# Unread products of the identity on TensorE at the stage borders of a two-layer decoder step

## The reference

```python
for l in range(DEPTH):                       # DEPTH = 2
    if l % 2 == 0:                           # gated linear recurrence and causal pooling
        hp, ... = hgrn_pool_mixer(yp, ...)
    else:                                    # sliding-window attention, 16 heads, 2 kv heads
        hp, ... = swa_mixer(yp, ...)
    yp = post_norm(yp, hp, ...)              # layer_norm(ALPHA * x + h)
    mk, mv = mem_kv(mem_prompt, mem_wkv[l])  # 256 memory tokens
    yp = post_norm(yp, cross_attn(yp, mk, mv, mem_wq[l], mem_wo[l]), ...)
    yp = post_norm(yp, peer_ffn(yp, ...), ...)
```

## Times and profile before

| | before |
|---|---|
| median of 3 runs | 2371.53 us (2364.65 to 2371.93) |
| the profiled execution's own time | 2373.22 us |
| its span | 2371.5 us |
| mean granted clock of TensorE over the span | 0.981 |
| PE busy | 2256.0 us, 95% |
| DVE busy | 1674.4 us, 71% |
| ACT busy | 1301.6 us, 55% |
| POOL busy | 1003.5 us, 42% |

### The profile page before, as it was taken

The page is one execution under the profiler, slowest core; times in us unless marked ns, Lnnn a source line. Parts: engine busy times, 40 slices in busy tenths (PEclk is TensorE's granted clock), DMA queues, the critical chain, the costliest instruction groups (busy, mean ns, idle before and its releaser), DMA issues. The chain is left out here.

```text
span 2371.5 us, 45604 instructions
## 1 busy us (share of the span) xinstructions
PE 2256.0 (95%) x15467; PEld 2039.7 (86%) x15467; DVE 1674.4 (71%) x3386; ACT 1301.6 (55%) x2953; POOL 1003.5 (42%) x777
## 2 busy tenths in 40 slices
PE   7899899999999999999989898999999999999998
PEld 7788699999999977888878787999999998778886
DVE  4667489969898656666646555899698884566666
ACT  4324365456776555555546544644677764555554
POOL 4604347997777610000033243499877774000000
PEclk9899999999999999999989999999999999999998
DMA  6738454444444565555544493444444446555553
GB/s 217 147 95 336 189 178 145 159 166 143 143 143 143 170 230 168 186 186 186 186 136 152 158 365 102 159 159 156 164 143 142 144 137 211 195 186 186 186 186 125
DMA packets 115506, 409.28 MB, mean 173 GB/s; under 512 B 20025, under 2 KB 22241, under 8 KB 110049
## 3 DMA queue, kind: packets, MB, share of 16 engines
q1 hardware_dynamic: 111328, 391.45, 49.2%
q0 software_dynamic: 4032, 15.86, 2.1%
HBM read 397.11 MB, written 10.14 MB: 172 GB/s over the span
## 5 line engine op out<-in xcount | busy, mean ns | idle before, releaser
L1986 POOL TENSOR_TENSOR slab_ring_lo<-slab_ring,u_hi 128x512 fp32r<-128x512 f32 x512 | 711.5, 1409 | 200.5 <-ACT u_hi L2080 199.5
L2028 PE MATMUL banks<-operand_hi,u_hi 128*128 128x264 f32 x2048 | 594.7, 290 | 18.5 <-POOL slab_ring_lo L1986 18.4
L2030 PE MATMUL banks<-operand_hi,slab_ring_lo 128*128 128x264 f32 x2048 | 583.1, 285 | 0.0
L2029 PE MATMUL banks<-operand_lo,u_hi 128*128 128x264 f32 x2048 | 582.0, 284 | 0.0
L308 POOL TENSOR_TENSOR slab_ring_lo<-slab_ring,slab_hi 128x512 fp32r<-128x512 f32 x130 | 174.8, 1346 | 691.2 <-ACT slab_hi L298 691.0
L2430 DVE TENSOR_TENSOR operand_lo<-slab_ring,operand_hi 128x512 fp32r<-128x512 f32 x512 | 352.7, 691 | 131.3 <-ACT operand_hi L2395 127.0
L2478 PE MATMUL banks<-operand_hi,w_hi 128*128 128x512 f32 x1024 | 410.2, 401 | 9.9 <-DVE w_lo L2426 9.9
L2080 ACT ACTIVATE u_hi<-slab_ring 128x512 fp32r<-128x512 f32 x512 | 321.8, 630 | 157.7 <-PE banks L2030 157.5
L2479 PE MATMUL banks<-operand_hi,w_lo 128*128 128x512 f32 x1024 | 408.0, 398 | 0.0
L2480 PE MATMUL banks<-operand_lo,w_hi 128*128 128x512 f32 x1024 | 407.8, 398 | 0.0
L2028 PEld LDWEIGHTS banks<-operand_hi,u_hi 128*128 128x128 f32 x2048 | 386.6, 189 | 23.1 <-POOL slab_ring_lo L1986 18.7
(11 more groups left out here) (400 smaller groups left out, 3943.0 us busy)
## 6 DMA issues: line engine op xcount, KB each, us to landing
slab_ring<-in_u SPq DMA_DIRECT2D x256, 512.0 KB, 3.3
slab_ring<-in_v SPq DMA_DIRECT2D x256, 512.0 KB, 3.3
slab_ring<-in_proj SPq DMA_DIRECT2D x144, 512.0 KB, 3.4
cache_k_T<-in_cache_k SPq DMA_DIRECT2D x16, 1024.0 KB, 8.8
cache_v<-in_cache_v SPq DMA_DIRECT2D x16, 1024.0 KB, 13.2
memory_T<-in_mem POOLq DMA_DIRECT2D x2, 1024.0 KB, 6.4
sample_state<-in_state POOLq DMA_DIRECT2D x1, 2048.0 KB, 13.2
out_mem_k_out<-mem_k_T SPq DMA_DIRECT2D x16, 128.0 KB, 3.4
```

Source lines behind the costliest of these rows:

```text
L1986: nc.gpsimd.tensor_tensor(step.ring_lo[:, s, g * HC:(g + 1) * HC, :], step.slab(s)[:, g * HC:(g + 1) * HC, :], hi[:, buf].bitcast(F32), AL ...
L2028: nc.tensor.matmul(bank, hi[:, buf, k, :], xh[:, c, :], start=(c == 0), stop=False)
L2029: nc.tensor.matmul(bank, hi[:, buf, k, :], xl[:, c, :], start=False, stop=False)
L2030: last = nc.tensor.matmul(bank, step.ring_lo[:, s, c, :], xh[:, c, :], start=False, stop=(c == DC - 1))
```

## The change

A new helper runs `count` products of the 128 x 128 identity with itself, in plain float32, into the first 128 columns of a bank of PSUM, each overwriting the one before. Nobody reads them. It is called in seven places of the code. Since `Fold` runs four times and the cross attention, `peer_up` and the norm twice, that makes thirteen places in TensorE's list, with 158 products. Six calls stand last in their block, the one in `token_norm` with 12 stands inside it. Five calls have a semaphore wait ahead, so that a bank is not overwritten while it is still read.

```diff
+    def keep_clock(self, bank, count):
+
+        for _ in range(count):
+            self.nc.tensor.matmul(self.ps[:, bank, 0:P], self.ident, self.ident, start=True, stop=True)
...
@@ Fold.tensor, at its end (out_mixer and out_cross, both layers)
+        pe.wait_ge(self.rstd_ready, 3)
+        step.keep_clock(MEAN_BANK, 9)
@@ mixer_attention, at the end of tensor's list (layer 0)
                 for k in range(13, 2 * DC):
                     memory(k)
+                pe.wait_ge(s_kv, 2 * SPREAD)
+                step.keep_clock(6, 14)
@@ window_sample, at the end (layer 1)
                 nc.tensor.transpose(ps[:, 4, 0:P], rows_o[:], step.ident).then_inc(s_oT, 1)
+                step.keep_clock(3, 14)
@@ cross_attention, at the end (both layers)
                 last.then_inc(s_sot, 1)
+                pe.wait_ge(s_e, 4)
+                step.keep_clock(0, 10)
@@ peer_up, at the end (both layers)
+            pe.wait_ge(s_g, NKEYS - 1)
+            step.keep_clock(0, 16)
@@ token_norm (12: both layers; 18: layer 0 alone)
             for j in range(HC):
                 nc.tensor.transpose(bank(j)[:, TP:T], z[2][:, j * P:(j + 1) * P], step.ident[0:TS, 0:TS])
+            step.keep_clock(5, 12)
             pe.wait_ge(s_z, 4)
...
+            if next_slab is not None:
+                pe.wait_ge(s_xa, 1)
+                step.keep_clock(4, 18)
```

## The result

The changed kernel is slower, by little but clear of the noise. Its median over 20 runs is 2376.89 us (2372.22 to 2382.70), beside 2367.65 us (2361.98 to 2375.46) for the kernel before in 20 runs on the same chip. The ratio is 1.0038 with a 95% interval of 1.0028 to 1.0048: +9.2 us, where +7.8 was forecast. The median lies in the range of 2370 to 2388.

What follows compares the result with a forecast made beforehand. TensorE was taken as the bound, losing time in waits at borders and at the lower clock. Delays of +14.9 us less gains of 5.1 and 2.0 gave +7.8 us, a median of 2379.3 us, range 2370 to 2388.

Steps and rivals of the forecast that it cites:

- The border waits for the products: At each border, the next stage opens 0.3 to 0.45 us after the last engine's work, TensorE's running matmuls included.
- a wrong sign to look for: At `mixer_attention`, `cross_attention` and `peer_up`, ACT or DVE start the next stage 0.3 to 0.45 us behind the added products.
- The price and the room: At each border, delay is 0.22 us per product (0.44 at half clock) less TensorE's time until the last other engine ends.
- Window and norm: Delays at the end of `window_sample`, 2.6 us, between full and half clock, and at layer 0's norm end, 0.3 us.
- the rival that the products run at the low clock themselves: `window_sample` costs 4.3 us, the norm 3.9, and the norm's gain of 1.65 is lost; +14.8, median 2386.3; chance 0.15.
- The gains that were counted on: Where products fill the pause: key scores 1.6 us, cross attention of layer 1 1.4, norm 1.65 plus 0.2 twice; 5.1 together.
- One of four borders held: Clock at `mixer_attention`, `window_sample` and both `peer_up` borders, worth 7.9 us together, one chance in four each: 2.0 us gained.
- the two `Fold` starts: Clock held at the `Fold` behind `mixer_attention` is worth 1.1 us, at the one behind `window_sample` 1.4 us.
- The clock holds over three microseconds: Rival: clock survives such pauses, so the four borders keep it; gains 13.0, net +1.9, 2373.4 us; chance 0.15.
- No clock is kept at all: Rival: products of the identity might not count as work; costs alone, +14.9, 2386.4 us; chance 0.07.

Runs made afterwards that it cites:

- dose: Changed kernel with 28 products at `mixer_attention` and `window_sample`, 0 and 20 at the cross attentions, 8 and 32 at `peer_up` by layer; one run, 2392.91 us.
- free_alone: Changed kernel without the products at the ends of `mixer_attention`, `window_sample`, `cross_attention` and `peer_up`; 2365.07 us, 0.9982 to the kernel before.
- three other small versions: Changed kernel with 7 per `Fold`, 12 and 14 in the norm; elsewhere counts cut to the room (window 6 or 2), or none; 0.9990, 0.9985, 0.9992 to the kernel before.
- costly_alone: Changed kernel with products only at the ends of `mixer_attention`, `window_sample`, `cross_attention` and `peer_up`, none in `Fold` and norm; 2387.46 us, 1.0078 to the kernel before.
- behind_again: Changed kernel with counts cut to the room, plus 10 products at each `Fold` start and 11 at `peer_down` start, behind the barrier; 2363.76 us, 0.9979 to the kernel before.

## Why the prediction was right

**The border waits for the products: right.** It is the step on which everything stood. ACT started 0.38 to 0.39 us behind the products' end at `mixer_attention` and `peer_up` at every count. At `cross_attention` the prediction named a wrong sign to look for (0.3 to 0.45 us): ACT starts 1.45 us behind there, and it does so with no product either, 1.41 us behind DVE's last copy (dose, layer 0):

```profile
282.84 0.27 DVE L1881 COPY mixed_T<-banks 128x64 f32<-128x64 f32 x1 [3.84 <-PE banks L1796]
284.52 1.15 ACT L303 ACTIVATE slab_hi<-slab_ring 128x512 fp32r<-128x512 f32 x2 [2.21 <-PEq L174]
```

Two barriers stand in a row at the end of that phase. The room was read from DVE's end, which is right all the same.

**The price and the room: right to a tenth of a microsecond at each border but two.** 0.22 us was taken for a product, 0.223 found. The figure of the Trainium skill, TensorE: Matmul & The Clock Gate, section Back-to-back issue gap, by which it would be an estimated 0.16, does not hold for this form: the 14 further ones at `mixer_attention` in the dose took 3.13 us, where it would have 2.2. The distances from the end of useful work to the next grew to 5.9, 6.1 and 6.7 us, forecast 6.0, 6.0 and 6.6.

**Window and norm: the place right, the size short.** 2.98 for 2.6 and 0.9 for 0.3. Both terms rest on how soon the clock comes back while the products run. At the window 14 took 4.39 us, where the full clock has 3.1 and the low one 6.2: they ran at the low clock until 1350.0 and at the full one from there. At the end of the norm 18 took 5.11 us, where 4.0 is the full clock: it was low until 1216.9, so the 12 products ahead had not kept it, as the sum assumed. So the rival that the products run at the low clock themselves was right for the first 2 us or so at both places, three to four tenths of its price, and wrong in the gain: behind the norm the clock was full, as forecast.

**The gains that were counted on: right.** Key scores 3.81 us in both layers, the pause at the cross attentions 0.4 us, the start of layer 1 at the full clock (worth 1.2 us in the profile, 1.65 in the sum). free_alone, which has these alone, is 4.6 us faster by its median; the terms give 5.1 less 0.8 for the `Fold` ends and 0.3 for the norm, 4.0. The three other small versions, which have the same gains and are hardly late, are 2.3 to 3.3 us faster, so the gains may be a little smaller than they were priced.

**One of four borders held: right as a chance, wrong in what it is worth.** In the profile `peer_down` of layer 1 kept the clock and was worth 2.8 us. Over the six kernels whose pause in front of `peer_down` is 3.08 to 3.17 us the clock held in three of twelve cases, the one in four that was given; behind the old pause of 4.00 us it fell in all eight. But the 2.5 us that were put on the two `Fold` starts (1.1 and 1.4) are no gain to be had: that step looked only at TensorE's time in the first product and at DVE's floor of 3.6 us, and never asked what POOL does when the product frees its slab sooner. At `mixer_attention` the clock fell, so the step was not put to the test there; behind the window it did hold through the first product, and that `Fold` took 61.4 us, 0.2 of it lateness, for 60.3: no gain, with DVE's seventh and eighth low parts at 1.5 us.

**The clock holds over three microseconds: mostly wrong.** In the changed kernel it fell within 1.1 us of the restart behind pauses of 2.80, 3.08, 3.72 and 3.87 us, held for 5.3 us behind the one of 2.85 at the window, and held behind one of 3.11:

```profile
1990.08 3.73 PE L187 MATMUL banks<-constants 128*128 128x128 f32 x32
1996.92 0.50 PE L2492 MATMUL banks<-operand_hi,w_hi 128*128 128x512 f32 x1 [3.11 <-DVE w_lo L2440]
```

So up to 3.1 us the length of the pause alone does not decide it: at 2.27 and at 3.08 (costly_alone, `peer_down`) one kernel's two layers differ. Over the 14 profiles here, past the first 15 us, pauses of 2.2 to 3.1 us go either way, and with every pause of 3.2 us or more the clock had fallen by 1.5 us behind its end or was low already.

**No clock is kept at all: wrong.** The mean clock rose from 0.981 to 0.989, and with the filler on both sides of the barrier to 0.993.

**What was luck.** The sum came within 1.4 us of the medians' difference, but not term by term: the costs were 0.9 us too low and the gains 0.7 too high, several stages that the forecast took as unchanged moved by 1 to 4 us in the profiles, and the one border in four that it counted on did hold. The mechanism is shown by the doses; that the sum fits so closely is partly chance.

## What to carry to other kernels

Filler that keeps a clock up is work like any other to a barrier. Ahead of it, count it against the time until the last other engine arrives, and stop there: of the nine at a `Fold` eight were free, and each one beyond the room cost 0.22 us for all five engines. The rest of the pause lies behind the barrier, so a filler for it belongs behind the barrier too; here it was worth some 3 us of 2370 on two chips, and showed no gain on the third. Before counting the clock as a gain, follow what the faster engine frees and who collides then.

## What the runs showed of the hardware

- A product of the identity in plain f32 (128 x 128 by 128 columns, two matmuls) costs 0.223 us in a stream at the full clock, and counts as work for the clock.
- The barrier at the end of a block waits for TensorE's running matmuls: the next block starts 0.38 to 0.45 us behind their end, with 8, 14, 28 or 32 products ahead of it (1.45 us where two barriers follow each other).
- A low half on DVE (128x264, two SBUF inputs) takes 0.42 us alone and 1.5 beside POOL's; POOL's (128x512) 1.27 alone and up to 2.4. Who wins changes from one profile to the next (58.31 and 62.49 us for a `Fold` with the same code up to there) and between the layers of one (82.48 and 85.4 us for `out_cross` in behind_again).
- A stage can be slower at the full clock, where that brings a collision about: 62.49 us at 1.00 against 59.52 with 3.4 us at 0.50.
- A start of `peer_down` with TensorE at the full clock waited up to 4.8 us, for something that comes from no engine, in the profiles from one chip and not at all in those from two others. The cause is open.
